# A decoder kernel's cross-attention: products in high and low parts, scaling on GpSimd, a new order of tiles

## The reference, cut to what matters

```python
def cross_attention(h, m, wq, wk, wv, wo):
    q = (h @ wq).reshape(B, S, X_HEADS, X_HEAD_DIM)      # 512 tokens, 4 heads of 256
    k = (m @ wk).reshape(B, M, X_HEADS, X_HEAD_DIM)      # 256 memory tokens
    v = (m @ wv).reshape(B, M, X_HEADS, X_HEAD_DIM)
    s = jnp.einsum('bshd,bmhd->bhsm', q, k).astype(jnp.float32) * (X_HEAD_DIM ** -0.5)
    p = jax.nn.softmax(s, axis=-1).astype(v.dtype)
    o = jnp.einsum('bhsm,bmhd->bshd', p, v).reshape(B, S, D_MODEL)
    return o @ wo
```

## Time and profile before

| what | value |
|---|---|
| median of 3 runs | 1712.34 us (1712.15 to 1712.43) |
| the profiled execution's own time | 1712.49 us |
| its span in the trace | 1710.7 us |
| mean granted TensorE clock | 0.998 of full speed |
| PE busy | 1685.8 us, 99% of the span |
| DVE, ACT, POOL busy | 652.3, 712.5, 819.2 us |

### The profile page before, as it was taken

One profiled execution on the slowest core, in us unless ns is written; L12 is line 12 of the kernel. 1 busy time (PEld: TensorE's weight loads), 2 busy tenths in 40 slices (PEclk: granted clock), 3 DMA queues, 4 the chain that ended last, 5 costly groups with the idle time before them and its releaser, 6 DMA issues.

```text
span 1710.7 us, 22973 instructions
## 1 busy us (share of the span) xinstructions
PE 1685.8 (99%) x9123; PEld 1364.2 (80%) x9123; DVE 652.3 (38%) x1413; ACT 712.5 (42%) x1367; POOL 819.2 (48%) x518
## 2 busy tenths in 40 slices
PE   8999999999999999999999999999999999999998
PEld 7888766887788888888878887768877888888886
DVE  3454675152263223311243456652431622232113
ACT  5425777262362222232353367764433612222322
POOL 4356668363134444455624467663632334443552
PEclk9999999999999999999999999999999999999999
DMA  6224112242122333232332340112421233222221
GB/s 204 94 91 137 50 26 51 74 149 99 37 75 99 99 98 99 74 111 90 122 99 84 105 138 26 26 51 87 160 74 51 86 98 99 91 96 84 99 98 74
DMA packets 101189, 154.13 MB, mean 90 GB/s; under 512 B 4396, under 2 KB 76380, under 8 KB 101084
## 3 DMA queue, kind: packets, MB, share of 16 engines
q1 hardware_dynamic: 97790, 147.09, 26.4%
q10 hardware_dynamic: 3294, 5.59, 1.0%
HBM read 150.56 MB, written 2.10 MB: 89 GB/s over the span
## 4 chain that ended last, share of the span: by engine, by line
PE 92%; ACT 3%; DVE 2%; DMA 1%; issue 1%; POOL 1%; DVEq 0%; SPq 0%; ACTq 0%
PE banks L1615 25%; PE banks L1617 25%; PE banks L1616 25%; PE banks L1885 4%; PE banks L1914 4%; PE banks L1938 4%; PE banks L2076 1%; PE banks L2058 1%; PE banks L1717 1%; ACT rows L855 1%; POOL w_lo L764 1%; PE banks L1645 1%; DVE banks L1267 1%; DVE h L1268 1%; PE banks L1934 0%
## 5 line engine op out<-in xcount | busy, mean ns | idle before, releaser
L764 POOL TENSOR_TENSOR w_lo<-raw,w_hi 128x1024 fp32r<-128x1024 f32 (+2 forms) x262 | 628.9, 2420 | 766.9 <-ACT w_hi L893 754.2
L893 ACT ACTIVATE w_hi<-raw 128x1024 fp32r<-128x1024 f32 (+2 forms) x264 | 259.5, 1027 | 728.1 <-PE banks L1617 713.2
L1615 PE MATMUL banks<-w_hi,a_lo 128*128 128x512 f32 (+1 forms) x864 | 332.6, 385 | 0.1
L1616 PE MATMUL banks<-w_lo,a_hi 128*128 128x512 f32 (+1 forms) x864 | 330.1, 382 | 0.0
L1617 PE MATMUL banks<-w_hi,a_hi 128*128 128x512 f32 (+1 forms) x864 | 330.0, 382 | 0.0
L1615 PE MATMUL banks<-a_hi,w_lo 128*128 128x512 f32 x768 | 299.5, 390 | 0.0
L1617 PE MATMUL banks<-a_hi,w_hi 128*128 128x512 f32 x768 | 298.8, 389 | 0.0
L1616 PE MATMUL banks<-a_lo,w_hi 128*128 128x512 f32 x768 | 298.8, 389 | 0.0
L1615 PEld LDWEIGHTS banks<-w_hi,a_lo 128*128 128x128 f32 x864 | 162.2, 188 | 33.3 <-issue 2.2
L1617 PEld LDWEIGHTS banks<-w_hi,a_hi 128*128 128x128 f32 x864 | 162.2, 188 | 31.4
L1616 PEld LDWEIGHTS banks<-w_lo,a_hi 128*128 128x128 f32 x864 | 162.3, 188 | 31.1 <-issue 0.5
(11 more groups left out here) (257 smaller groups left out, 2347.2 us busy)
## 6 DMA issues: line engine op xcount, KB each, us to landing
raw<-in_ffn_w_up SPq DMA_DIRECT2D x44, 1024.0 KB, 5.1
raw<-in_ffn_w_down SPq DMA_DIRECT2D x20, 1024.0 KB, 4.9
raw<-in_w_in SPq DMA_DIRECT2D x19, 1024.0 KB, 5.1
raw<-in_x_wk SPq DMA_DIRECT2D x8, 1024.0 KB, 5.3
raw<-in_x_wv SPq DMA_DIRECT2D x8, 1024.0 KB, 4.9
raw<-in_x_wq SPq DMA_DIRECT2D x8, 1024.0 KB, 5.1
raw<-in_x_wo SPq DMA_DIRECT2D x8, 1024.0 KB, 4.9
raw<-in_cmp_wk SPq DMA_DIRECT2D x4, 1024.0 KB, 5.4
```

Of the source, the lines that this page charges most:

```text
L764: inc(pool.tensor_tensor(lo_half(u, half), raw_half(u, half), hi_half(u, half).bitcast(F32), ALU.subtract), lo_made, n)
L893: inc(act.activation(hi_half(u, half), raw_half(u, half), ACT.Copy), hi_made)
L1615: pe.matmul(dst, st_lo, mv_hi, start=first, stop=False)
L1616: pe.matmul(dst, st_hi, mv_lo, start=False, stop=False)
```

## The change

It touches the cross-attention of both layers, in seven ways.

1. Scores and values are made by `three`. Keys, values, queries and transposed probabilities each get a high part (`xk_hi`, `xv_hi`, `xq_hi`, `xpT_hi`, all by ACT) and a low part (`xk_lo` by POOL, the others by DVE).
2. The scaling of probabilities (`xscale`) moves from DVE to POOL, all 16 ahead of the low halves of output unit 1. DVE keeps the reciprocal.
3. Score tiles 0 and 1 (`XEARLY`) are made before the last query piece, the loop starts at step 2.
4. PE's waits for a query bank are one bank at a time (`xq_bank`), not two.
5. Three banks of output unit 0 (`XO_STEPS`, `xo_unit_0`) are made in steps 17, 19 and 21, and `rows_gemm` makes the other five.
6. ACT casts output unit 1 in steps 16 and 17 instead of before the loop.
7. ACT makes the first four row parts before the cast of query unit 0, not after it.

The new tiles lie in memory that other tiles of the same layer have done with.

```diff
+XEARLY = 2
+XO_STEPS = {17: 1, 19: 2, 21: 0}
...
+                def xk_rest():
+                    pool.wait_ge(xk_hi_made.sem, xk_hi_made.at(l, 1))
+                    inc(pool.tensor_tensor(xk_lo[:], xkT[:], xk_hi[:].bitcast(F32), ALU.subtract), xk_lo_made)
+                def xscale(i):
+                    pool.wait_ge(xrdened.sem, xrdened.at(l, i + 1))
+                    inc(pool.tensor_scalar(xprob[:, i % XPROBS, :], xprob[:, i % XPROBS, :], rden[:, i % 8:i % 8 + 1], 1.0, ALU.mult, ALU.mult), xscaled)
                 for u in range(UNITS):
+                    if u == U_OUT + RING:
+                        xk_rest()
+                    if u == U_XO + 1:
+                        for i in range(16):
+                            xscale(i)
...
+                act.wait_ge(xk_ready.sem, xk_ready.at(l, 8))
+                inc(act.activation(xk_hi[:], xkT[:], ACT.Copy), xk_hi_made)
                 cast_to(U_OUT + 4)
                 post_and_pre(0, 1, (U_XV + 1, U_XV + 1, U_XV + 1, U_XV + 2, U_XV + 3))
+                hi_parts(range(4))
                 cast_to(U_XQ + 1)
-                hi_parts(range(4))
                 for b in range(4):
                     wait_xv(act, l, b)
-                    inc(act.activation(xv[:, b // 2, 512 * (b % 2):512 * (b % 2) + 512], bank(b), ACT.Copy), xv_ready)
+                    inc(act.activation(xv_hi[:, b // 2, 512 * (b % 2):512 * (b % 2) + 512], bank(b), ACT.Copy), xv_hi_made)
                 hi_parts(range(4, KD))
                 cast_to(U_XQ + 2)
                 act.dma_start(gain_row[:], row_broadcast(norm_x_post, l)).then_inc(gain_landed[1].sem, 16)
-                cast_to(U_XO + 2)
+                def xq_part(m):
+                    wait_cols(act, l, xq_psum, m // 2, U_XQ + m // 2, m % 2)
+                    inc(act.activation(xq_hi[:, m, :], bank(m % 4), ACT.Copy, scale=256 ** -0.5), xq_hi_made)
...
+                for m in range(6):
+                    xq_part(m)
+                    if m % 2:
+                        cast_to(U_XQ + m // 2 + 3)
+                xq_part(6)
+                for i in range(XEARLY):
+                    xexp(i)
+                xq_part(7)
...
+                    inc(act.activation(xpT_hi[:, head % 2, :, P * t:P * t + P],
+                                       bank(4 - i % 2, MEM).rearrange("p (m q) -> p m q", m=2), ACT.Copy), xpT_hi_made)
+                for i in range(XEARLY, XSTEPS + 1):
                     if i < 16:
-                        act.wait_ge(xmaxed.sem, xmaxed.at(l, i + 1))
-                        if i >= XPROBS:
-                            act.wait_ge(xpT_psum.sem, xpT_psum.at(l, i - XPROBS + 1))
-                        inc(act.activation(xprob[:, i % XPROBS, :], bank(i % 3, MEM), ACT.Exp,
-                                           bias=neg_max[:, i % 8:i % 8 + 1], accum_out=den[:, i % 8:i % 8 + 1]), xexped)
+                        xexp(i)
+                    if i in (16, 17):
+                        cast_halves(2 * U_XO + i - 13)
...
-                lo_parts()
-                for m in range(KD):
-                    wait_cols(dve, l, xq_psum, m // 2, U_XQ + m // 2, m % 2)
-                    inc(dve.tensor_scalar(xqT[:, m, :], bank(m % 4), 256 ** -0.5, None, ALU.mult), xq_ready)
-                def xscale(i):
+                lo_parts(range(4))
+                for b in range(4):
+                    dve.wait_ge(xv_hi_made.sem, xv_hi_made.at(l, b + 1))
+                    part = (slice(None), b // 2, slice(512 * (b % 2), 512 * (b % 2) + 512))
+                    inc(dve.tensor_tensor(xv_lo[part], bank(b), xv_hi[part].bitcast(F32), ALU.subtract), xv_lo_made)
+                lo_parts(range(4, KD))
+                def xq_part(m):
+                    dve.wait_ge(xq_hi_made.sem, xq_hi_made.at(l, m + 1))
+                    inc(dve.scalar_tensor_tensor(xq_lo[:, m, :], bank(m % 4), 256 ** -0.5, xq_hi[:, m, :].bitcast(F32), ALU.mult, ALU.subtract), xq_lo_made)
+                def xmax(i):
+                    dve.wait_ge(xs.sem, xs.at(l, i + 1))
+                    inc(dve.tensor_reduce(neg_max[:, i % 8:i % 8 + 1], bank(i % 3, MEM), AX.X, ALU.max, negate=True), xmaxed)
+                def xrecip(i):
                     dve.wait_ge(xexped.sem, xexped.at(l, i + 1))
-                    r = rden[:, i % 8:i % 8 + 1]
-                    link(dve.reciprocal(r, den[:, i % 8:i % 8 + 1]))
-                    inc(dve.tensor_scalar(xprob[:, i % XPROBS, :], xprob[:, i % XPROBS, :], r, None, ALU.mult), xscaled)
-                for i in range(XSTEPS + 1):
+                    inc(dve.reciprocal(rden[:, i % 8:i % 8 + 1], den[:, i % 8:i % 8 + 1]), xrdened)
+                def xpT_rest(i):
+                    head, t = divmod(i, 4)
+                    part = (slice(None), head % 2, slice(None), slice(P * t, P * t + P))
+                    dve.wait_ge(xpT_hi_made.sem, xpT_hi_made.at(l, i + 1))
+                    inc(dve.tensor_tensor(xpT_lo[part], bank(4 - i % 2, MEM).rearrange("p (m q) -> p m q", m=2),
+                                          xpT_hi[part].bitcast(F32), ALU.subtract), xpT_lo_made)
+                for m in range(7):
+                    xq_part(m)
+                for i in range(XEARLY):
+                    xmax(i)
+                for i in range(XEARLY):
+                    xrecip(i)
+                xq_part(7)
+                for i in range(XEARLY, XSTEPS + 1):
                     if i < 16:
-                        dve.wait_ge(xs.sem, xs.at(l, i + 1))
-                        inc(dve.tensor_reduce(neg_max[:, i % 8:i % 8 + 1], bank(i % 3, MEM), AX.X, ALU.max, negate=True), xmaxed)
-                    if 1 <= i <= 16:
-                        xscale(i - 1)
+                        xmax(i)
+                    if XEARLY <= i - 1 < 16:
+                        xrecip(i - 1)
+                    if 0 <= i - XLAG_T < 16:
+                        xpT_rest(i - XLAG_T)
...
+                        if ahead:
+                            ahead(m)
...
                     for c in range(2):
-                        ins = pe.matmul(bank(i % 3, MEM), xqT[:, 2 * head + c, P * t:P * t + P], xkT[:, 2 * head + c, :],
-                                        start=c == 0, stop=c == 1)
+                        q, tokens = 2 * head + c, slice(P * t, P * t + P)
+                        ins = three(bank(i % 3, MEM), xq_hi[:, q, tokens], xq_lo[:, q, tokens], xk_hi[:, q, :], xk_lo[:, q, :], c == 0, c == 1)
...
+                def xq_bank(u, m):
+                    if u < 2:
+                        pe.wait_ge(xv_lo_made.sem, xv_lo_made.at(l, 2 * u + m + 1))
+                    else:
+                        pe.wait_ge(xq_lo_made.sem, xq_lo_made.at(l, 2 * (u - 2) + m + 1))
+                    if (u, m) == (3, 1):
+                        for i in range(XEARLY):
+                            xscores(i)
+                for u in range(4):
+                    cols_gemm(U_XQ + u, 2 * (u % 2), xq_psum, None if u else 1, lambda m: xq_bank(u, m))
...
                     if i >= 2:
-                        pe.wait_ge(xpT_ready.sem, xpT_ready.at(l, i - 1))
+                        pe.wait_ge(xpT_lo_made.sem, xpT_lo_made.at(l, i - 1))
                     for m in range(2):
-                        ins = pe.transpose(bank(3 + i % 2, P, P * m), xprob[:, i % XPROBS, P * m:P * m + P], ident[:])
+                        ins = pe.transpose(bank(4 - i % 2, P, P * m), xprob[:, i % XPROBS, P * m:P * m + P], ident[:])
...
-                        ins = pe.matmul(bank(5 + j % 3), xv[:, m, P * j:P * j + P], xprobT[:, head % 2, m, :],
-                                        start=m == 0, stop=m == 1)
+                        cols = slice(P * j, P * j + P)
+                        ins = three(bank(5 + j % 3), xv_hi[:, m, cols], xv_lo[:, m, cols], xpT_hi[:, head % 2, m, :], xpT_lo[:, head % 2, m, :],
+                                    m == 0, m == 1)
...
+                def xo_unit_0(b):
+                    hi, lo = unit(U_XO)
+                    rest(U_XO)
+                    pe.wait_ge(xexped.sem, xexped.at(l, 16 if b == 0 else 13 + b))
+                    pe.wait_ge(xo_lo.sem, xo_lo.at(l, 2))
+                    t, n = divmod(b, 2)
+                    st, nn = slice(P * t, P * t + P), slice(512 * n, 512 * n + 512)
+                    for k in range(2):
+                        three(bank(b), a_hi[:, k, st], a_lo[:, k, st], hi[:, k, nn], lo[:, k, nn], k == 0, False)
+                for i in range(XEARLY, XSTEPS):
                     if i < 16:
                         xscores(i)
                     if 0 <= i - XLAG_T < 16:
                         xtransposes(i - XLAG_T)
                     if i in XPIECES:
                         xvalues(XPIECES[i])
+                    if i in XO_STEPS:
+                        xo_unit_0(XO_STEPS[i])
...
-                rows_gemm(U_XO, 4, 1, lambda i: pe.wait_ge(xo_lo.sem, xo_lo.at(l, 2 * i + 2)), xo_bank)
```

(47 more changed lines are left out.)

21 lines of the change are left out of this document (14 added, 7 removed).

## The result

The changed kernel takes 1721.82 us (median; 1721.29 to 1722.26) against 1712.24 for the kernel before on the same chip: ratio 1.0056, 95% interval 1.0043 to 1.0068. It is 9.6 us slower, where 4.3 us faster were forecast, and it lies outside the range. The profiled execution has a span of 1719.5.

A forecast was written before the change was run, and what follows sets the result against it. PE, busy 99% of the span, bounds the kernel before; a DVE-ACT ring would pace the changed loop. Profiled 1712.49 - 2 x 1.64 - 1.05 = 1708.2, hence 1708.0 us as median; range 1704.0 to 1712.5.

The forecast's parts named there:

- part 4: Ends of the cross-attention stage: layer 1's wait before query products goes, 1.05 us once; moved casts and splits cost nothing.
- With the cover gone it costs what is missing: Layer 2's moved cast: first GpSimd half ends some 0.5 us before PE wants it; costed at nothing.
- The signs: Profile after: maxima 1.66 us apart, PE idle 0.5 to 0.8 before transposes, stage 35.0, no wait before query transposes.
- Parts 2 and 3: Cross-attention: a DVE-ACT wait loop sets the pace; stage lasts 35.0 us, net gain 1.64 a layer.
- the ring: Score loop: DVE maximum, ACT exponential, ACT copy, DVE low-part subtract wait on each other in a closed loop, 1.66 us a turn.
- Part 1: Cross-attention scores and value products: three passes instead of float32 save 5.1 us of PE work a layer.
- PE alone would need 1.14 a step: Score loop: PE's 0.72 score tile, 0.22 transposes and 0.2 type changes make 1.14 us a step.
- the second rival: Score loop: PE's own work sets the stage, 31.8 us instead of 35.0, time 1701.6; 8 in 100.
- the wait of 1.05 before the query products: Layer 1: PE's wait for ACT's copies of the memory values goes, saving 1.05 us once.
- Scaling on GpSimd: Score loop: scaling takes 0.55 us with 0.6 to spare, costs nothing; rival that it binds, 1715.7, 3 in 100.
- GpSimd's last long subtracts: Rival, beside last low parts: two 2.36 us subtracts hold up DVE, up to 2.4 a layer, 1712.8; 6 in 100.
- Output products: Late loop steps 17, 19, 21: output work of 4.08 us taken from the next stage fills only the last short waits.

The follow-up runs named there:

- e1_cast_split: Changed kernel with the cast of the last memory-value unit put back ahead of the high parts, the first query unit's cast still behind them: 1708.07 us.
- e2_reorder_alone: Kernel before, with only the high parts moved ahead of the call casting the last memory-value unit and first query unit: 1725.74 us.
- e9_before_cast_split: Kernel before, with the high parts put between the casts of the last memory-value unit and the first query unit: 1710.89 us.
- e5_float32_rest_kept: Changed kernel with e1_cast_split's cast order, but scores and value products plain float32 again, without high and low parts: 1705.85 us.
- e4_copy_first: e1_cast_split with ACT copying transposes i-3 before the exponential of i, not behind it: 1696.09 us.
- e10_extra_maximum_ring: e1_cast_split with one more 128x256 maximum on DVE ahead of each low part of the transposed probabilities, result unused: 1716.81 us.

## Why the prediction was wrong

The step that failed is in part 4: "Now the high parts go ahead of the cast." I took from the earlier trace rows that the call ahead of them casts one unit, the one whose transfer had just landed. It casts up to the first query unit, and the last memory-value unit is among what it has left to do. In the kernel before, that unit's halves were cast while PE still made its earlier products and so cost nothing (its transposes start at 360.46):

```profile
357.16 2.00 ACT L893 ACTIVATE w_hi<-raw 128x1024 fp32r<-128x1024 f32 x2
```

Behind the high parts they can't begin before PE's transposes are done, and PE has nothing else then. "With the cover gone it costs what is missing" was weighed for the query unit alone; for the value unit 4.57 us were missing in each layer. e1_cast_split, e2_reorder_alone and e9_before_cast_split show it from three sides. The sum lacked this term altogether, and the slower passes that came with it: 1708.0 and 13.75 are 1721.8. The signs by which the prediction wished to be told right came true in the main, and the time was off all the same: they too looked past this place.

Point by point:
- **Parts 2 and 3**, the ring and the stage: right, with 1.65 for 1.66 and 34.87 for 35.0, and the low part of 0.42 without a row measured 0.42. With the failed step mended the time is 1708.07, where 1708.0 stood.
- **Part 1**, PE's saving: e5_float32_rest_kept against e4_copy_first gives 9.8 us for the passes with their changes of type. The prediction had 10.2 for the passes alone, and took off 0.2 a step, 6.4 in all, for the changes. That term was mis-sized. The estimate "PE alone would need 1.14 a step" was too high, since the pair of transposes and its changes of type take 0.24, not 0.42 (0.94 a step, less six passes of 0.117). The ring hid this, so it moved no forecast but that of the second rival: 1701.6 there, 1696.09 measured.
- **Part 4**, the wait of 1.05 before the query products: it went, and no wait for the query unit's late cast or for the split keys stands in e1_cast_split's list of PE's waits.
- **Scaling on GpSimd** didn't bind: 0.48 us. The Trainium skill, GPSIMD Engine Reference, "Engine selection", has that engine about two times slower than VectorE with two inputs and at roughly line rate with one; this one-input scaling takes 0.48 against 0.35, 1.4 times as long.
- **GpSimd's last long subtracts** held nothing up. In layer 1 they run from 448.55 for 4.76 us, and the DVE low parts beside them take 0.42 and 0.69 as elsewhere. By the rule of the Trainium skill, SBUF — State Buffer, "SBUF: two separate sides", they were to go free, since one input lies in PSUM; the trace agrees.
- **Rivals.** None was the cause. That a longer ring costs PE time is confirmed by e10_extra_maximum_ring; 2 x 11 times the growth is a fair size for it, but only because two errors nearly cancel, and the slower clock comes on top. My rivals all looked at the loop; none asked what the moved call was holding ahead of PE.
- **Output products**: no run takes them back in the ring, where PE's timeline of e1_cast_split has no wait beside them; in the open order they fill 1.6 us a layer.

What stays open: why the clock comes back after 5 us in layer 1 and after 2.7 in layer 2. The 1.5 us by which e2_reorder_alone exceeds its sum go with the clock: its traced execution (1724.07) is at the sum, with a mean granted clock of 0.996, and the other three (1725.22 to 1726.61) have 0.994; where in them it was lower, no trace shows. No run separates the wait from the slower clock behind it; their shares are read from the trace alone. The one-bank waits of PE and the later casts of output unit 1 were not taken back by themselves.

## What to carry to other kernels

When a call of the form "cast up to n" is moved, list the instructions that it issues at that place, from the order of both kernels, and ask of each when PE wants it: a counter hides how many there are. Before work is given to a second engine to save PE time, close the loop of waits between in-order engines and divide its length by the number of steps that it spans; here a copy put ahead of an exponential on ACT was worth 12 us, more than the cheaper products themselves (9.8). An estimate for a bound that another bound hides should be checked once that other is gone.

The best of these kernels is e4_copy_first: 1696.09 us, 0.95% below the kernel before.

## What the hardware did that I had not expected

A wait on PE cost more than its length. After 4.57 us without work the granted clock stood at its lower level, and passes of 128x512 came 0.43 us apart instead of 0.23 for 5 us (layer 1) and 2.7 us (layer 2): 2.65 and 1.61 us beyond the waits, for the most part by these passes. It need not fall within the wait: in e2_reorder_alone, layer 1, it was at full speed through 4.58 us and fell just after. Nor does the longest wait tell alone. In e10_extra_maximum_ring, layer 1, waits of 0.87 us with 1.1 us of work between them were followed by about 3 us of slow passes, and one of 1.85 us later on was not; in layer 2 the same waits of 0.87 were not, and one of 1.83 was. So equal waits at equal places had unequal outcomes, and a forecast can only give such a term a range. In the changed kernel's own ring, with waits of 0.54 and a single one of 1.3, the stage ran at full clock.
